# A float32 three-layer kernel: its first loads in another order on two queues, its first weight unit in smaller pieces, two copies moved to ScalarE

## The reference, cut to what matters

```python
u = rms_norm(h, g_mix[layer])                # h = x, 256 x 1024
proj = u @ w_in                              # 1024 x 2208
h = h + mla_stick_breaking_mixer(u, ...)     # h is needed again later (residual)
```

## Time and profile before

| | |
|---|---|
| median of 3 runs | 1077.72 us (1077.44 to 1077.78) |
| span of the profiled execution | 1076.1 us |
| around its span, median less span | 1.6 us |
| TensorE busy | 1059.5 us, 98% |
| VectorE, ScalarE, GpSimd busy | 755.1, 575.8, 207.5 us |
| first product of weight unit 0 | at 11.72 us |

### The profile page before, as it was taken

One profiled execution on the slowest core, in us unless ns is written; L12 is line 12 of the kernel. 1 busy time (PEld: TensorE's weight loads), 2 busy tenths in 40 slices (PEclk: granted clock), 3 DMA queues, 4 the chain that ended last, 5 costly groups with the idle time before them and its releaser, 6 DMA issues.

```text
span 1076.1 us, 22251 instructions
## 1 busy us (share of the span) xinstructions
PE 1059.5 (98%) x8808; PEld 1026.7 (95%) x8808; DVE 755.1 (70%) x1238; ACT 575.8 (54%) x853; POOL 207.5 (19%) x189
## 2 busy tenths in 40 slices
PE   9999999999999999999999999999999999999997
PEld 7998899999999889999999999999899999999997
DVE  6778665655757776656556589988988658877652
ACT  5668554444545565644445454447667355565542
POOL 0432030000220000300000287885450000000000
PEclk9999999999999999999999999999999999999999
DMA  9735366656675343566555745553345535554451
GB/s 277 217 111 174 102 190 190 192 171 205 219 240 190 125 157 114 180 188 193 173 176 185 219 128 176 153 172 118 118 127 171 173 118 195 194 181 144 158 182 40
DMA packets 187941, 181.32 MB, mean 168 GB/s; under 512 B 17951, under 2 KB 186284, under 8 KB 187867
## 3 DMA queue, kind: packets, MB, share of 16 engines
q1 hardware_dynamic: 187179, 177.94, 52.2%
q0 software_dynamic: 544, 2.10, 0.7%
q10 hardware_dynamic: 144, 0.26, 0.1%
HBM read 179.24 MB, written 1.05 MB: 168 GB/s over the span
## 4 chain that ended last, share of the span: by engine, by line
PE 86%; DVE 6%; ACT 5%; issue 2%; POOL 1%; DVEq 0%; ACTq 0%
PE ps L572 27%; PE ps L573 26%; PE ps L577 26%; DVE w_lo L397 2%; ACT w_hi L381 2%; DVE ps L2714 1%; PE ps L1880 1%; PE ps L2054 1%; PE ps L2247 1%; PE ps L2063 1%; PE ps L567 1%; POOL w_lo L409 1%; PE ps L1849 0%; PE ps L1801 0%; PE ps L1873 0%
## 5 line engine op out<-in xcount | busy, mean ns | idle before, releaser
L397 DVE TENSOR_TENSOR w_lo<-raw,w_hi 128x2048 fp32r<-128x2048 f32 (+3 forms) x157 | 333.4, 2137 | 138.3 <-ACT w_hi L381 138.0
L381 ACT ACTIVATE w_hi<-raw 128x2048 fp32r<-128x2048 f32 (+3 forms) x182 | 316.3, 1753 | 31.4 <-PE ps L577 21.4
L572 PE MATMUL ps<-u_hi,w_hi 128*128 128x256 f32 x944 | 265.4, 281 | 0.4 <-DVE w_lo L2435 0.4
L573 PE MATMUL ps<-u_lo,w_hi 128*128 128x256 f32 x944 | 261.5, 277 | 0.0
L577 PE MATMUL ps<-u_hi,w_lo 128*128 128x256 f32 x932 | 258.2, 277 | 0.0
L572 PE MATMUL ps<-m_hi,w_hi 128*128 128x258 f32 (+2 forms) x792 | 228.4, 288 | 1.2 <-POOL w_lo L409 0.5
L573 PE MATMUL ps<-m_lo,w_hi 128*128 128x258 f32 (+2 forms) x792 | 224.7, 284 | 0.0
L577 PE MATMUL ps<-m_hi,w_lo 128*128 128x258 f32 (+2 forms) x786 | 223.0, 284 | 0.0
L572 PEld LDWEIGHTS ps<-u_hi,w_hi 128*128 128x128 f32 x944 | 177.7, 188 | 3.0 <-issue 1.9
L573 PEld LDWEIGHTS ps<-u_lo,w_hi 128*128 128x128 f32 x944 | 177.4, 188 | 0.2
L577 PEld LDWEIGHTS ps<-u_hi,w_lo 128*128 128x128 f32 x932 | 175.1, 188 | 0.0
(11 more groups left out here) (372 smaller groups left out, 1636.5 us busy)
## 6 DMA issues: line engine op xcount, KB each, us to landing
raw<-in_w_in SPq DMA_DIRECT2D x24, 1024.0 KB, 5.3
raw<-in_w_gate SPq DMA_DIRECT2D x22, 1024.0 KB, 5.4
raw<-in_w_up SPq DMA_DIRECT2D x22, 1024.0 KB, 5.4
raw<-in_ffn_up SPq DMA_DIRECT2D x22, 1024.0 KB, 5.1
raw<-in_w_down SPq DMA_DIRECT2D x16, 768.0 KB, 4.8
raw<-in_od_w_qkv SPq DMA_DIRECT2D x12, 1024.0 KB, 5.7
raw<-in_w_down SPq DMA_DIRECT2D x16, 640.0 KB, 4.4
raw<-in_ev_w_in SPq DMA_DIRECT2D x7, 1024.0 KB, 10.2
```

The lines of the kernel that those rows point to most:

```text
L381: nc.scalar.activation(w_hi[t % RING][:, 0:n], raw[t % RAW][:, 0:n], ACT.Copy).then_inc(hi_done, 1)
L397: nc.vector.tensor_tensor(w_lo[t % RING][:, 0:n], raw[t % RAW][:, 0:n], w_hi[t % RING][:, 0:n].bitcast(F32), ALU.subtract).then_inc(lo_don ...
L572: nc.tensor.matmul(out_ap, a_h, b_h, start=start and n == 0, stop=False)
L573: nc.tensor.matmul(out_ap, a_h, b_l, start=False, stop=False)
```

## The change

- SP issues the first half of x first and the identity second. The second half of x and the mix gains leave SP's list and are issued by ScalarE, ahead of its table load.
- The first half of unit 0 comes in two loads of 256 KB, each with a semaphore of its own, and is split by ScalarE and VectorE in two pieces of 512 columns. TensorE waits for piece 0 ahead of `kt` 0 and for piece 1 ahead of `kt` 2.
- The gains are turned into bank 6 instead of 7, and the two products of ones behind that transpose now stand ahead of the wait for `mix_ready`.
- ScalarE copies tiles 0 and 1 to `h`, each behind the u_lo of its tile, ahead of piece 0; VectorE no longer does. ScalarE makes u_hi 3 between the two pieces.
- VectorE's order becomes u_lo 0, 1, piece 0, u_lo 2, piece 1, u_lo 3, 4, second half, u_lo 5 to 7.
- TensorE runs three products of ones instead of one behind the transposes of x, and waits for u_lo 0 and 1 there instead of 0 to 2.

```diff
@@ SP
-        nc.sync.dma_start(gain_rows[0:16, :], g_mix.rearrange(...)).then_inc(sem("mix_landed"), 16)
-        for b in range(2):
-            nc.sync.dma_start(x_rows[:, b, :], x[0, b * P:(b + 1) * P, :]).then_inc(sem(f"x_landed{b}"), 16)
+        nc.sync.dma_start(x_rows[:, 0, :], x[0, 0:P, :]).then_inc(sem("x_landed0"), 16)   # ahead of the identity
...
-        nc.sync.dma_start(pw(slot, KT, UC)[:, 0:KT // 2, :], first[:, 0:KT // 2, :]).then_inc(sem("half_landed"), 16)
+        for n in range(2):
+            nc.sync.dma_start(pw(slot, KT, UC)[:, 2 * n:2 * n + 2, :], first[:, 2 * n:2 * n + 2, :]).then_inc(sem(f"piece_landed{n}"), 16)
@@ ScalarE
+        nc.scalar.dma_start(x_rows[:, 1, :], late_rows).then_inc(sem("x_landed1"), 16)
+        nc.scalar.dma_start(gain_rows[0:16, :], g_mix.rearrange(...)).then_inc(sem("mix_landed"), 16)
         act.preload_act_table_set("natural_log_exp_and_others")
...
         for kt in range(3):
             x_hi(kt)
-        act.wait_ge(sem("half_landed"), 16)
-        nc.scalar.activation(w_hi[0][:, 0:HALF], raw[0][:, 0:HALF], ACT.Copy).then_inc(sem("half_hi"), 1)
-        for kt in range(3, KT):
+        for kt in range(2):
+            act.wait_ge(sem("xl_done"), split_at["mix0"] + kt + 1)
+            nc.scalar.activation(h[:, kt, C1], x_bank(kt), ACT.Copy).then_inc(sem("h_act"), 1)
+        piece_hi(0)
+        x_hi(3)
+        piece_hi(1)
+        for kt in range(4, KT):
             x_hi(kt)
@@ TensorE
-        nc.tensor.transpose(ps[:, 7, 0:16], gain_rows[0:16, :], ident[0:16, 0:16]).then_inc(sem("mix_turned"), 1)
+        nc.tensor.transpose(ps[:, 6, 0:16], gain_rows[0:16, :], ident[0:16, 0:16]).then_inc(sem("mix_turned"), 1)
+        keep_busy(2)
         pe.wait_ge(sem("mix_ready"), 1)
-        keep_busy(2)
...
-        keep_busy()
-        for kt in range(3):
+        keep_busy(3)
+        for kt in range(2):
             pe.wait_ge(sem("xl_done"), split_at["mix0"] + kt + 1)
             keep_busy()
-        pe.wait_ge(sem("half_lo"), 1)
-        pe.wait_ge(sem("h_copied"), 2)
+        pe.wait_ge(sem("h_act"), 2)
         for kt in range(KT):
-            if kt == KT // 2:
+            if kt in (0, 2):
+                pe.wait_ge(sem("piece_lo"), kt // 2 + 1)
+            elif kt == KT // 2:
                 pe.wait_ge(lo_done, 1)
@@ VectorE
-        for kt in range(2):
-            x_lo(kt)
-            h_copy(kt)
+        x_lo(0)
+        x_lo(1)
+        piece_lo(0)
         x_lo(2)
...
+        piece_lo(1)
+        x_lo(3)
+        x_lo(4)
         dve.wait_ge(hi_done, 1)
```

More of the change, by code:

```diff
@@ L411, in split_lo_pool @@
         a.then_inc(lo_done, 1)
-    LATENT, HALF = 5, UNIT // 2
+    LATENT, HALF, PIECE = 5, UNIT // 2, UNIT // 4
     def latent_parts(to, of):
@@ L1075, in load_down @@
             load(ph, i, k, src(i + k // 8, k // 4 % 2, k % 4), nk=DOWN_KT[k % 4][1])
+    late_rows = x[0, P:2 * P, :]
     block = ctx.enter_context(nc.Block())
@@ L1095, in _ @@
         early, idents = where["rot32"][0], P
+        nc.sync.dma_start(x_rows[:, 0, :], x[0, 0:P, :]).then_inc(sem("x_landed0"), 16)
         nc.sync.dma_start(const[:, 0:idents], constants[:, 0:idents]).then_inc(sem("ident_landed"), 16)
-        nc.sync.dma_start(gain_rows[0:16, :], g_mix.rearrange("a (r p) -> (a r) p", p=P)).then_inc(sem("mix_landed"), 16)
-        for b in range(2):
-            nc.sync.dma_start(x_rows[:, b, :], x[0, b * P:(b + 1) * P, :]).then_inc(sem(f"x_landed{b}"), 16)
         w = ev_w_in[0]
@@ L1303, in _ @@
     def _(act):
+        nc.scalar.dma_start(x_rows[:, 1, :], late_rows).then_inc(sem("x_landed1"), 16)
+        nc.scalar.dma_start(gain_rows[0:16, :], g_mix.rearrange("a (r p) -> (a r) p", p=P)).then_inc(sem("mix_landed"), 16)
         act.preload_act_table_set("natural_log_exp_and_others")
@@ L1310, in x_hi, with piece_hi @@
             nc.scalar.activation(u_hi[:, kt, 0:T1], x_bank(kt), ACT.Copy, scale=gains[:, g:g + 1]).then_inc(sem("xh_done"), 1)
+        def piece_hi(n):
+            cols = slice(n * PIECE, (n + 1) * PIECE)
+            act.wait_ge(sem(f"piece_landed{n}"), 16)
+            nc.scalar.activation(w_hi[0][:, cols], raw[0][:, cols], ACT.Copy).then_inc(sem("piece_hi"), 1)
         for kt in range(3):
             x_hi(kt)
-        act.wait_ge(sem("half_landed"), 16)
-        nc.scalar.activation(w_hi[0][:, 0:HALF], raw[0][:, 0:HALF], ACT.Copy).then_inc(sem("half_hi"), 1)
-        for kt in range(3, KT):
+        for kt in range(2):
[5 more added lines that the diff above has]
+        for kt in range(4, KT):
             x_hi(kt)
@@ L1321, in _ @@
         act.wait_ge(sem("xl_done"), split_at["mix0"] + 3)
-        nc.scalar.activation(h[:, 2, C1], ps[:, 2, 0:T1], ACT.Copy).then_inc(sem("h_third"), 1)
+        nc.scalar.activation(h[:, 2, C1], ps[:, 2, 0:T1], ACT.Copy).then_inc(sem("h_act"), 1)
         for b in range(2):
@@ L1801, in keep_busy @@
                 nc.tensor.matmul(ps[:, 7, 0:T1], log_ms[:, 0:P], log_ms[:, 0:T1], start=True, stop=True)
-        pe.wait_ge(sem("idle_rows"), 1)
+        pe.wait_ge(sem("eps_ready"), 2)
         keep_busy(2)
@@ L1818, in row_turns @@
             pe.wait_ge(sem("rows_landed"), 16 * 15)
-            pe.wait_ge(sem("h_copied"), KT - 1)
+            pe.wait_ge(sem("h_copied"), KT - 3)
             nc.tensor.transpose(ps[:, 6, 0:GAIN_ROWS], gain_rows[:], ident[0:GAIN_ROWS, 0:GAIN_ROWS])
@@ L1835, in root_rows @@
             pe.wait_ge(sem("const_landed"), 16)
-            pe.wait_ge(sem("h_copied"), 3)
+            pe.wait_ge(sem("h_copied"), 1)
             for b in range(2):
@@ L1958, in _ @@
             if k == 1:
-                pe.wait_ge(sem("h_third"), 1)
+                pe.wait_ge(sem("h_act"), 3)
             elif k == 2:
-                pe.wait_ge(sem("h_copied"), KT - 1)
+                pe.wait_ge(sem("h_copied"), KT - 3)
             block_unit(k, 16 * k, k in (2, 8))
@@ L2413, in _ @@
         nc.vector.memset(eps[:, 0:1], EPS).then_inc(sem("eps_ready"), 1)
-        nc.vector.memset(log_ms[:], 1.0).then_inc(sem("idle_rows"), 1)
+        nc.vector.memset(log_ms[:], 1.0).then_inc(sem("eps_ready"), 1)
         dve.wait_ge(sem("mix_turned"), 1)
-        nc.vector.tensor_copy(gains[:, 0:16], ps[:, 7, 0:16]).then_inc(sem("mix_ready"), 1)
+        nc.vector.tensor_copy(gains[:, 0:16], ps[:, 6, 0:16]).then_inc(sem("mix_ready"), 1)
         dve.wait_ge(sem("mix_ready"), 1)
@@ L2428, in h_copy, with piece_lo @@
             nc.vector.tensor_copy(h[:, kt, C1], x_bank(kt)).then_inc(sem("h_copied"), 1)
-        for kt in range(2):
-            x_lo(kt)
-            h_copy(kt)
-        x_lo(2)
[L2434 to L2438, removed]
+        def piece_lo(n):
+            cols = slice(n * PIECE, (n + 1) * PIECE)
+            dve.wait_ge(sem("piece_hi"), n + 1)
+            nc.vector.tensor_tensor(w_lo[0][:, cols], raw[0][:, cols], w_hi[0][:, cols].bitcast(F32), ALU.subtract)\
+                .then_inc(sem("piece_lo"), 1)
+        x_lo(0)
+        x_lo(1)
+        piece_lo(0)
+        x_lo(2)
+        piece_lo(1)
+        x_lo(3)
+        x_lo(4)
         dve.wait_ge(hi_done, 1)
@@ L2441, in _ @@
             .then_inc(lo_done, 1)
-        for kt in range(6, KT):
+        for kt in range(5, KT):
             x_lo(kt)
```

## The result

| | before | after |
|---|---|---|
| median | 1077.9 us (6 runs) | 1081.37 us (6 runs) |
| ratio, 95% interval | | 1.0033 [1.0023, 1.0044] |
| span of the profiled execution | 1076.1 us | 1080.0 us |
| first x_hi on ScalarE (t0) | 8.02 | 11.09 |
| first product of unit 0 | 11.72 | 14.32 |

Slower by 3.5 us, 0.3%. The last row says where to look: from the third unit on the two executions take the same time, so the whole difference of 3.9 us between the spans stands in the first 28 us. (The profiled execution was the longest of the six, 1081.88.)

The account below looks back on a forecast made before the run. TensorE, busy 98% of 1076.1 us, was taken as the bound, with only its early gaps changeable. Later t0 (+2.2) and a longer chain behind it (+1.0) gave span 1079.3, plus 1.6 around it 1080.9 us; range 1078.4 to 1082.3.

Parts of the forecast that it names:

- Loads: Opening loads: x's last half lands at 5.91, gains and identity 0.19 us behind; TensorE has both at about 6.0.
- the bound of 6.84: Opening loads: latest time for identity and gains, if the earlier issue of x gives nothing.
- Clock and t0: TensorE ahead of ScalarE's first x_hi: idle leaves it at 1.2 GHz, rise about 9.7; t0 10.2 instead of 8.02, +2.2.
- Behind t0: From first x_hi to third unit: ScalarE's h copies and pieces lengthen 15.73 to +16.7, so +1.0 us.
- The stall in unit 0: TensorE in the middle of the first unit: waits 1.2 us for the second half's w_lo, which eats the 0.5 gained.
- The sum: Whole kernel: 2.2 + 1.0 = 3.2 us more, span 1079.3, median 1080.9.
- Rival A: Opening loads: two queues bring x sooner, t0 9.0, sum +2.0, 1079.7 us; chance 0.18.
- Rival B: Wait before gains' transpose: small loads pass large ones and land by 3.6, t0 7.15, 1077.8 us; chance 0.10.
- Rival C: From t0 to third unit: nothing lengthens, the +1.0 falls to near 0, +2.2, 1079.9 us; chance 0.12.
- nothing takes up earlier weights: SP's weight loads: weights come some 0.4 to 0.9 us earlier, without gain, as ScalarE reaches each later than before.

Follow-up runs that it names:

- loads_back: Changed kernel, but SP issues all loads in the old order (identity, gains, both x halves): 1078.02 us, 1.0002 to before.
- no_ones: Changed kernel without the two products of ones between the gains' transpose and x: 1080.03 us, 1.0020 to before.
- h_vector: Changed kernel, but the copies of tiles 0 and 1 to h are VectorE's again: 1080.46 us, 1.0023 to before.
- loads_only: Kernel before with only the loads changed (SP: first x half, identity; ScalarE: second x half, gains): 1080.86 us, 1.0027 to before.
- one_queue: Changed kernel, but SP issues all four loads: both x halves, identity, gains: 1081.17 us, 1.0030 to before.
- ones_only: Kernel before with only the gains turned into bank 6 and the two ones ahead of the wait for the gains' copy: 1077.54 us, 0.9999.
- mix_act_h: Changed kernel, h copies of tiles 0 and 1 on VectorE, identity then x halves from SP, gains from ScalarE: 1077.69 us, 1.0000 to before.
- ones_mix_act: Kernel before with the ones ahead of the gains' copy wait and the gains issued by ScalarE: 1077.26 us, 0.9997 to before.
- small_on_act: Changed kernel, but ScalarE issues identity and gains and SP both x halves: 1080.30 us, 1.0020 to before.
- loads_back_h: Changed kernel with all loads from SP in the old order and the copies of tiles 0 and 1 on VectorE: 1077.78 us, 1.0001 to before.

## Why the prediction was right, point by point

- *Slower, by place.* Forecast 1080.9, measured 1081.4. The loss stands where it was put: TensorE waits for identity and gains behind x, and the ones, which filled a wait before, stand in series. loads_back and no_ones show each half of it.
- *Loads.* The mis-sized term. Identity and gains were to be there at 6.0; the transpose ran at 6.88, just past the bound of 6.84. x itself came at 6.36 instead of 5.91, and the identity 0.5 behind that, where I had 72 KB at full rate, 0.19. The first part is largely this execution, the slowest of its six: with the same loads x was there at 5.95, 6.05 and 6.15 and the small transpose ran at 6.49, 6.59 and 6.64 (no_ones, h_vector, loads_only). The second part is 0.5 in all four, and one_queue shows it without a second queue, 0.84. A small load's landing isn't its bytes over the rate when others are in flight.
- *Clock and t0.* From the small transpose to t0 I had 4.2 us and it took 4.21. So t0 came at 11.09 (+3.07) and not at 10.2 (+2.2), by the loads alone. The rise came at about 10.9, 4.0 behind the small transpose where I had carried over 3.7 from the kernel before; the ninth transpose had begun by then, so it made no difference.
- *Behind t0.* +1.0 forecast, +0.84 measured: first product at +3.23 (+3.2), the half's w_lo at +6.96 (+7.11), the second unit at +10.48 (+10.56), the third at +16.57 (+16.7). The stall in unit 0 was 0.80 and not 1.2: w_lo came 0.15 earlier, and the idle time counts from the end of the product ahead of it (17.30, +6.21), where I had added up spacings to +6.0. That most of the growth is the copies, and not the pieces, is shown by h_vector.
- *The sum.* +3.9 in the profiled spans, +3.5 in the medians, against +3.2: the loads' +0.9 and the chain's -0.2. With the small transpose at 6.5 to 6.6, as in the three other profiles with these loads, the loads' error is 0.5 to 0.6, which fits the medians better (an estimate).
- *Rival A* (x sooner on two queues) is out: x came later than on one. *Rival B* named the right point, landing before or after about 4: loads_back, with an early landing, measures 1078.0 where B had 1077.8. That small loads pass large ones didn't happen (one_queue: 6.48 and 6.65 behind 5.81). *Rival C* is out by the +0.84.
- *What I missed.* I wrote that nothing takes up earlier weights. That held for the changed kernel, but I hadn't read how closely ScalarE followed the second unit's landing in the kernel before (12.87 behind 12.83). An x that came earlier would have been worth little: in ones_only and mix_act_h t0 is 0.75 and 0.99 earlier than before, the third unit 0.11 and 0.22. In loads_back, B's case, the copies in ScalarE's line fill most of that time, and 0.17 us of waiting for the unit are left. It didn't touch the forecast, because in the changed kernel everything came later.

## What to carry to other kernels

Before a small load is moved behind or beside a large one, ask who waits for both: the first operation here needed 72 KB of identity and gains, and half a microsecond of lead over the large loads brought them in 2 to 4 us sooner. Filler work that is free in a wait becomes part of the chain when the wait moves ahead of it. And before the head of a chain is pulled forward, look for the next landing on it: here the second weight unit landed less than 0.1 us before it was needed, so an earlier x gained almost nothing.

## What the runs showed of the hardware

- A 64 KB load and an 8 KB load landed 2.0 and 1.9 us after issue with 0.46 us of lead over x (ones_mix_act), 4.3 and 4.1 when issued at the same time on another queue (small_on_act), and 4.8 and 4.5 (one_queue) or 5.6 and 5.4 (after) behind x.
- One queue delivered the two halves of x at 4.46 and 5.81 (one_queue), two queues at 6.06 and 6.36 (after; in no_ones, the earliest, at 5.66 and 5.95): the pair was not sooner, only more alike. The weights were issued from 2.70 on in the first case and from 1.75 on in the second, and no run separates the two.
- The rise of TensorE's clock differs between profiles with the same TensorE instructions ahead of it. In loads_back eight transposes from 5.54 took 1.07 us, all at 2.4 GHz; in loads_back_h, with the same loads and ones, sixteen from 5.56 took 3.11, most of them at 1.2 GHz:

```profile
5.56 3.11 PE L1821 MATMUL ps<-const,x_rows 128*128 128x128 f32 x16
```

t0 is 7.21 in the one and 7.72 in the other. That is more than the medians of these two kernels differ, so t0 of a single profile is not to be read to a tenth.
